# A second inner product of the convolution groups computed in divided form

## The chip, the core and the metric

The kernel runs on one NeuronCore of a Trainium2 chip. TensorE (PE) multiplies matrices into PSUM; its weight loads are shown apart (PEld). VectorE (DVE), ScalarE (ACT) and GpSimd (POOL) work elementwise, and SyncE's queue (SP) issues the DMAs. Engines run beside each other and wait for one another only through semaphores. The metric is the device time of one execution in microseconds, the median of a few runs.

## The reference

One layer of a decoder trunk on 1024 tokens of width 1024, in float32. The projection `h @ w_in` gives twelve blocks of 1024 columns; those of the convolution branch are `c_a`, `x_a`, `z_a`, `b_a`:

```python
u = c_gate * xv
u = conv(u, conv_w) + conv_b      # causal, depthwise, 3 taps over positions
y = b_gate * u * silu(z)
y_a = y @ w_a_out
# beside it: retention over 4 heads, then
merged = sigmoid(g_a) * y_a + sigmoid(g_b) * y_b
x = x + merged @ w_o              # and a final RMSNorm
```

## The kernel before, in words

Every float32 operand is split into a high part (a cast by ScalarE) and a low part (the rest, a subtraction by VectorE), and each product is three matmuls: high x high, high x low, low x high.

The projection runs in 28 value units and then 20 *groups* `g` of channels: groups 0, 1, 18, 19 for gates, 2 to 9 (`CONVS`) for the convolution, 10 to 17 (`turn`) for q and k. A group is a 2x2 block product done with seven products in place of eight, in the order `ORDER = (1, 6, 2, 5, 7, 3, 4)`. Each product is a *unit*: its weights are cast and split into one of three slots (`slots`, taken in turn), so the unit three places later waits until a unit's matmuls are done. A full unit has 24 matmuls of 128x512. GpSimd makes the weight sums of the next group (`s1`, `s3`, `s2`, `s4`) from quadrants that SP loads; product 6 needs S2, and S4 waits for product 6's low part. After each product VectorE adds the PSUM result to running sums (`add`), and the next product in the same banks waits for that (product 5 waits for the addition of 6).

In groups 1 to 18 (`TWICE`) product 4 is itself divided the same way (`second_units`): two half units with 18 and 24 matmuls of 128x256. GpSimd makes four weight sums of 128x256 for the second half (`second_sums`), and VectorE needs four more additions (`second_first`, `second_rest`), because the small products go to several quarters of the result.

For convolution group `g` the elementwise work runs while TensorE is in group `g + 1`: VectorE makes two halves of `u` (`conv_product`; the second half, `conv_product(g, 1)`, still in group g), three taps (`conv_tap`, the first a `TENSOR_SCALAR`), the gating (`conv_y`), and in the group itself an early gate product (`conv_early`) that product 7 waits for; ScalarE makes sigmoids; GpSimd three gate products (`conv_gate`).

The order on each engine is the order in which its loop is written: loops over unit places `u`, in which place `p` of group `g` runs the additions of the unit before, then the high or low part of the unit two places on, then the rest. Nothing reorders it.

Of the kernel before, what the change touches and what calls it, by code (L numbers as in the profile page):

```python
# [6 lines left out]
F32 = mybir.dt.float32  # L7
# [5 lines left out]
P = 128  # L13
# [37 lines left out]
UNIT_TABLE = [(g, p) for g in range(GROUPS) for p in range(8 if g in TWICE else 7)]  # L51
# [54 lines left out]
def ended_at(g):  # L106

    return unit_at(g, 4) + (g in TWICE)


def columns_of(u):

    return 3 * QUARTER if u >= VALUE_UNITS and place_of(u)[0] in TWICE and place_of(u)[1] == 6 else 2 * HALF
# [7 lines left out]
def summed_until(g):  # L121

    return 16 + 4 * g + 4 * len([n for n in TWICE if n < g])


def second_summed(g, n):

    return summed_until(g) + 4 + n


def second_added(g, n):

    return 20 + 4 * (g - TWICE.start) + n
# [138 lines left out]
def build(nc, x_t, columns, w_value, w_channel, w_last, x_rows, final_g, rope, tables, identity, out):  # L272
# [7 lines left out]
    kept_d = nc.dram_tensor("kept_scratch", (P, 2, 2, QUARTER), F32, kind="Internal").ap()  # L280
# [24 lines left out]
    t4_sums = sb("t4_sums", CONS_AT + 8 * KB, [P, 4, 2, QUARTER])  # L305
    v_d, v_b, v_a, v_c = (sb(f"value_{r}", WORK_AT + n * 8 * KB, [P, 2, 1024]) for n, r in enumerate("dbac"))
# [110 lines left out]
    final_in, row_squared, row_var, row_scaled = ident_in, squared, var_made, kept_scaled  # L417

# [33 lines left out]
    def t4_part(n, part):  # L452

        return hc[:, KEPT_AT[4], part, 2 * (n // 2):2 * (n // 2) + 2, n % 2 * QUARTER:(n % 2 + 1) * QUARTER]

    def second_part(name, part):
        return t4_part(1, part) if name == "T3" else hx[:, ("T1", "T2", "T4").index(name), part]

    def second_bank(g):

        return set_at(g + 1, 6)
# [31 lines left out]
    def _(sp):  # L493
# [147 lines left out]
        for part in range(2):  # L641
            sp.dma_start(kept_d[:, part], t4_part(1, part).bitcast(F32)).then_inc(x_in[4], 16)
        for g in range(GROUPS):
            if g + 1 < GROUPS:
# [3 lines left out]
            if g == TWICE.stop:  # L648
                sp.wait_ge(unit_done, ended_at(g - 1) + 1)
                for part in range(2):  # L650
                    sp.dma_start(t4_part(1, part).bitcast(F32), kept_d[:, part]).then_inc(x_in[4], 16)
            if g + 1 < GROUPS:
# [194 lines left out]
    def _(pool):  # L847
# [50 lines left out]
        def second_sums(g):  # L898

            d = work[ROLES[g]["d"]]  # L900
            a11, a12, a22, a21 = (d[:, n * QUARTER:(n + 1) * QUARTER] for n in range(4))
# [1850 lines left out]
```

## Time and profile before

| what | value |
|---|---|
| median of 3 runs | 1368.03 us (1367.47 to 1368.32) |
| profiled execution, first to last instruction | 1366.5 us |
| TensorE, VectorE, ScalarE, GpSimd busy | 99%, 78%, 43%, 35% of the span |
| weight loads busy | 83% |
| granted TensorE clock, mean | 0.999 |

The profile is of one execution. Its view by timeline lists instructions by their start; neighbours of one line are merged, and the bracket says how long the engine was idle before and what ended that. A matmul's shown duration is longer than its distance to the next one, since they are pipelined: read the distances of the starts. On VectorE and ScalarE the next instruction's start is shown a little before the last one's end.

### The profile page before, as it was taken

Reading aid. Unit: us, or ns where it says so; the run is one execution under the profiler, and the core shown is the slowest. Engines: PE = TensorE matmul, PEld = TensorE weight load, DVE = VectorE, ACT = ScalarE, POOL = GpSimd, SP = SyncE. Lnnn points to the kernel's source line nnn. Section 1 sums busy time; section 2 is a strip of 40 time slices with the busy share of each in tenths; the row PEclk is TensorE's granted clock in tenths of the full one; section 3 lists DMA queues with packets and bytes.
Section 4 is the critical chain, followed back from the end, with each engine's and each line's share of the span. In section 5 each row is a group of like instructions: output and inputs, shape, how many; then the busy total and the mean of one; then the engine's idle time right before and its main releaser. Section 6 shows DMA issues by size and latency. Waiting matters only on the chain.

```text
span 1366.5 us, 16902 instructions
## 1 busy us (share of the span) xinstructions
PE 1354.6 (99%) x6498; PEld 1138.4 (83%) x6498; DVE 1063.1 (78%) x1053; ACT 591.4 (43%) x801; POOL 473.3 (35%) x349
## 2 busy tenths in 40 slices
PE   9999999999999999999999999999999999999997
PEld 7888888888888888888888888888888888888886
DVE  6898474578877777788888888747776998788887
ACT  7843233323222233234333333438778434433445
POOL 0100232244555554555555666415454001100002
PEclk9999999999999999999999999999999999999999
DMA  9746313322212222355443444657767699945443
GB/s 338 215 128 216 114 56 124 124 77 77 77 50 63 74 62 62 109 154 154 138 140 124 116 146 141 198 193 254 264 229 261 142 327 312 233 164 200 161 86 124
DMA packets 106128, 212.74 MB, mean 156 GB/s; under 512 B 6977, under 2 KB 49089, under 8 KB 101185
## 3 DMA queue, kind: packets, MB, share of 16 engines
q1 hardware_dynamic: 103024, 193.82, 42.4%
q0 software_dynamic: 2880, 17.83, 6.6%
q8 instruction: 52, 0.85, 0.3%
q14 instruction: 28, 0.22, 0.0%
q10 hardware_dynamic: 144, 0.02, 0.0%
HBM read 148.20 MB, written 55.05 MB: 149 GB/s over the span
## 4 chain that ended last, share of the span: by engine, by line
PE 95%; issue 1%; ACT 1%; DVE 1%; POOL 1%; DMA 0%; SPq 0%; POOLq 0%; DVEq 0%; ACTq 0%
PE psum L2488 16%; PE psum L2489 16%; PE psum L2486 16%; PE psum L2623 7%; PE psum L2625 7%; PE psum L2624 7%; PE psum L2413 4%; PE psum L2415 4%; PE psum L2416 4%; PE psum L2430 2%; PE psum L2432 2%; PE psum L2431 2%; PE psum L2531 2%; PE psum L2533 2%; PE psum L2532 2%
## 5 line engine op out<-in xcount | busy, mean ns | idle before, releaser
L2488 PE MATMUL psum<-hc,slots 128*128 128x512 f32 x976 | 379.8, 389 | 0.0
L2486 PE MATMUL psum<-hc,slots 128*128 128x512 f32 x976 | 379.8, 389 | 0.0
L2489 PE MATMUL psum<-hc,slots 128*128 128x512 f32 x976 | 379.8, 389 | 0.0
L1088 ACT ACTIVATE slots<-work 128x1024 fp32r<-128x1024 f32 (+1 forms) x158 | 162.0, 1036 | 435.9 <-PE psum L2489 329.0
L1583 DVE TENSOR_TENSOR slots<-work,slots 128x1024 fp32r<-128x1024 f32 (+1 forms) x158 | 228.6, 1448 | 39.0 <-ACT slots L1088 39.0
L2489 PEld LDWEIGHTS psum<-hc,slots 128*128 128x128 f32 x976 | 183.2, 188 | 38.1
L2486 PEld LDWEIGHTS psum<-hc,slots 128*128 128x128 f32 x976 | 183.2, 188 | 37.5
L2488 PEld LDWEIGHTS psum<-hc,slots 128*128 128x128 f32 x976 | 183.2, 188 | 37.3
L1348 ACT ACTIVATE last_slot<-arena 128x1024 fp32r<-128x1024 f32 x112 | 118.6, 1062 | 163.0 <-PE psum L2625 156.8
L2623 PE MATMUL psum<-last_slot 128*128 128x512 f32 (+1 forms) x452 | 175.3, 388 | 0.0
L2625 PE MATMUL psum<-last_slot 128*128 128x512 f32 (+1 forms) x452 | 175.0, 387 | 0.0
L2624 PE MATMUL psum<-last_slot 128*128 128x512 f32 (+1 forms) x452 | 175.0, 387 | 0.0
L1900 DVE TENSOR_TENSOR last_slot<-arena,last_slot 128x1024 fp32r<-128x1024 f32 x112 | 135.7, 1222 | 30.4 <-ACT last_slot L1348 29.8
L2624 PEld LDWEIGHTS psum<-last_slot 128*128 128x128 f32 x452 | 84.9, 188 | 17.4
L2625 PEld LDWEIGHTS psum<-last_slot 128*128 128x128 f32 x452 | 84.9, 188 | 17.4
L2623 PEld LDWEIGHTS psum<-last_slot 128*128 128x128 f32 x452 | 84.9, 188 | 17.2
L903 POOL TENSOR_TENSOR work<-work 128x256 f32<-128x256 f32 x18 | 16.3, 906 | 234.7 <-DVE slots L1583 234.7
L2413 PE MATMUL psum<-slots,hc 128*128 128x512 f32 x224 | 88.2, 394 | 1.3 <-DVE slots L1583 1.3
L2416 PE MATMUL psum<-slots,hc 128*128 128x512 f32 x224 | 87.2, 389 | 0.0
L2415 PE MATMUL psum<-slots,hc 128*128 128x512 f32 x224 | 87.2, 389 | 0.0
L878 POOL TENSOR_TENSOR work<-work,work 128x1024 f32<-128x1024 f32 x20 | 48.3, 2414 | 95.8 <-DVE slots L1583 95.8
L1729 DVE TENSOR_TENSOR tp_v<-psum,tp_v 128x1024 f32<-128x1024 f32 x40 | 48.7, 1218 | 35.9 <-PE psum L2489 35.9
(214 smaller groups left out, 2331.2 us busy)
## 6 DMA issues: line engine op xcount, KB each, us to landing
work<-w_channel SPq DMA_DIRECT2D x80, 512.0 KB, 3.7
arena<-w_last SPq DMA_DIRECT2D x19, 1024.0 KB, 7.5
qk<-qk_scratch SPq DMA_DIRECT2D x32, 512.0 KB, 3.4
arena<-w_last POOLq DMA_DIRECT2D x9, 1024.0 KB, 11.4
v_raw<-value_scratch SPq DMA_DIRECT2D x32, 256.0 KB, 3.7
arena<-gate_scratch SPq DMA_DIRECT2D x16, 512.0 KB, 7.1
value_c<-w_value SPq DMA_DIRECT2D x10, 512.0 KB, 4.8
rows_of_x<-x_rows SPq DMA_DIRECT2D x8, 512.0 KB, 8.8
```

What stands on the lines that cost most here:

```text
L1088: nc.scalar.activation(slots[:, u % SLOTS, 0, 0:columns_of(u)], src, ACT.Copy).then_inc(w_hi, 1)
L1583: nc.vector.tensor_tensor(slot[:, 1, :], src, slot[:, 0, :].bitcast(F32), ALU.subtract).then_inc(w_ready, 1)
L1900: nc.vector.tensor_tensor(slot[:, 1, :, :], pair_at(group, product, j), slot[:, 0, :, :].bitcast(F32), ALU.subtract).then_inc(last_ready, 1)
L2413: nc.tensor.matmul(bank, x_high, w_high, start=product in starts and i == 0 and kk == 0, stop=False, skip_group_check=True)
L2415: nc.tensor.matmul(bank, x_high, w_low, start=False, stop=False, skip_group_check=True)
L2416: last = nc.tensor.matmul(bank, x_low, w_high, start=False, stop=i == 1 and kk == 1, skip_group_check=True)
L2486: nc.tensor.matmul(bank, slot[:, 0, w], x_high, start=product in STARTS and j == 0, stop=False, skip_group_check=True)
L2488: nc.tensor.matmul(bank, slot[:, 0, w], x_low, start=False, stop=False, skip_group_check=True)
L2489: last = nc.tensor.matmul(bank, slot[:, 1, w], x_high, start=False, stop=j == 3, skip_group_check=True)
L2623: nc.tensor.matmul(bank, l_high, r_high, start=start, stop=False, skip_group_check=True)
L2624: nc.tensor.matmul(bank, l_high, r_low, start=False, stop=False, skip_group_check=True)
L2625: return nc.tensor.matmul(bank, l_low, r_high, start=False, stop=stop, skip_group_check=True)
```

## The change

In convolution groups (`THIRDS = CONVS`) product 3 is divided as product 4 is. The unit table gets one more place there, `THIRD_HALF`, and the halves alternate: first of 3, first of 4, second of 3, second of 4. `second_units` becomes `first_half` and `second_half`, for either product. GpSimd makes four more weight sums, VectorE four more additions. Before group 2, VectorE and ScalarE make the sums and differences of the quarters of product 3's activations once (`t3_quarter`, `t_sum`, `third_high`, `third_low`, four of each); one quarter is overwritten by them, so SP stores it and loads it back before group 10.

Elementwise work moves: the first tap with the bias goes to ScalarE (`first_tap`); the last tap and the gating go ahead of product 7's low part; `conv_product(g, 1)` goes behind the low part of the next group's product 6; the second sigmoid (`late_gate`) goes ahead of that product's cast. On SP the store of `y` goes ahead of one weight load.

```diff
-UNIT_TABLE = [(g, p) for g in range(GROUPS) for p in range(8 if g in TWICE else 7)]
+THIRDS = CONVS
+LAST_HALF, THIRD_HALF = 7, 8
+UNIT_TABLE = [(g, p) for g in range(GROUPS) for p in (0, 1, 2, 3, 4, 5, 6, THIRD_HALF, LAST_HALF)
+              if (p != THIRD_HALF or g in THIRDS) and (p != LAST_HALF or g in TWICE)]
...
+def third_ended_at(g):
+
+    return VALUE_UNITS + UNIT_TABLE.index((g, THIRD_HALF if g in THIRDS else 5))
+
+
+def halved_product(g, product):
+
+    return product == 4 and g in TWICE or product == 3 and g in THIRDS
+
+
+def product_at(n):
+
+    return 3 if n == THIRD_HALF else ORDER[min(n, 6)]
 
 
...
+            if g == THIRDS.start:
+                stores[kind_of(g - 1)](g - 1)
...
-                sp.wait_ge(w_ready, unit_at(g, 3) + 1)
+                if g in THIRDS and g > THIRDS.start:
+                    stores[kind_of(g - 1)](g - 1)
+                sp.wait_ge(w_ready, third_ended_at(g) + 1)
                 load_work(g + 1, "c", 1)
-            if g:
+            if g and g not in THIRDS:
                 stores[kind_of(g - 1)](g - 1)
...
+            if g in THIRDS:
+                second_sums(g, 3)
             if g in TWICE:
-                second_sums(g)
+                second_sums(g, 4)
...
+        def late_gate(g):
+
+            after(g, 3)
+            nc.scalar.activation(gate_z[:, HALF:T], tp_first[g % 2][:, 1, :], ACT.Sigmoid).then_inc(z_sig, 1)
+
+        def first_tap(g):
+
+            c = g - CONVS.start
+            act.wait_ge(conv_step, 5 * c + 3)
+            if c:
+                act.wait_ge(y_out, 16 * c)
+            nc.scalar.activation(taps[:, :], u_pad[:, 0:T], ACT.Identity, scale=cols[:, KT + c:KT + c + 1],
+                                 bias=cols[:, (1 + CONV) * KT + c:(1 + CONV) * KT + c + 1]).then_inc(conv_step, 1)
 
...
+            if VALUE_UNITS <= u < UNITS and place_of(u)[1] == LAST_HALF and place_of(u)[0] in THIRDS:
+                late_gate(place_of(u)[0])
             if u + 2 < UNITS:
                 high(u + 2)
...
+            if p == 1 and g - 1 in CONVS:
+                first_tap(g - 1)
...
-            if n == 0:
-                if c:
-                    dve.wait_ge(y_out, 16 * c)
-                nc.vector.tensor_scalar(taps[:, :], u_pad[:, 0:T], conv_col(0, c), conv_col(CONV, c), ALU.mult, ALU.add)\
-                    .then_inc(conv_step, 1)
-            else:
-                nc.vector.scalar_tensor_tensor(taps[:, :], u_pad[:, n:n + T], conv_col(n, c), taps[:, :],
-                                               ALU.mult, ALU.add).then_inc(conv_step, 1)
+            nc.vector.scalar_tensor_tensor(taps[:, :], u_pad[:, n:n + T], conv_col(n, c), taps[:, :],
+                                           ALU.mult, ALU.add).then_inc(conv_step, 1)
 
...
-                if n == 6 and g in TWICE:
-                    second_first(g)
-                elif n == 7:
-                    second_rest(g)
+                if n in (5, 6) and halved_product(g, product_at(n)):
+                    second_first(g, product_at(n))
+                elif n == LAST_HALF:
+                    second_rest(g, 4)
                     low(u + 1)
+                    if g in THIRDS:
+                        conv_product(g, 1)
                     add(g, 4)
+                elif n == THIRD_HALF:
+                    second_rest(g, 3)
+                    add(g, 3)
                 elif ORDER[n] not in (1, 2):
                     add(g, ORDER[n])
 
-            if u + 2 < UNITS and (u < VALUE_UNITS or place_of(u)[1] < 7):
+            if u >= VALUE_UNITS and place_of(u)[1] == 2 and place_of(u)[0] - 1 in CONVS:
+                conv_tap(place_of(u)[0] - 1, 2)
+                conv_y(place_of(u)[0] - 1)
+            if u + 2 < UNITS and (u < VALUE_UNITS or place_of(u)[1] != LAST_HALF):
                 low(u + 2)
...
-                        conv_tap(last, 0)
                         conv_tap(last, 1)
-                    if p == 2:
-                        conv_tap(last, 2)
-                        conv_y(last)
...
-                if p == 6:
-                    conv_product(g, 1)
...
+        def first_half(g, product):
+
+            u, z = unit_at(g, product), second_bank(g, product)
             pe.wait_ge(w_ready, u + 1)
-            pe.wait_ge(sum_made, 5 * g + sums_until(ORDER, 7))
-            if g == TWICE.start:
+            pe.wait_ge(sum_made, 5 * g + sums_until(ORDER, before(ORDER, product)))
+            if product == 4 and g == TWICE.start:
                 pe.wait_ge(h_ready, made(3) + 4)
-            product_of_quarters(u, 0, quarter(0), one_six, start=True)
-            product_of_quarters(u, 1, quarter(2), c11)
-            product_of_quarters(u, 2, second("T4"), c21).then_inc(unit_done, 1)
-            pe.wait_ge(w_ready, u + 2)
-            product_of_quarters(u + 1, 2, second("T1"), five, start=True)
-            product_of_quarters(u + 1, 3, second("T3"), seven, start=True)
-            product_of_quarters(u + 1, 1, quarter(3), c12)
-            pe.wait_ge(value_sum, second_added(g, 1))
-            product_of_quarters(u + 1, 0, second("T2"), one_six).then_inc(unit_done, 1)
+            if product == 3:
+                pe.wait_ge(sum_made, 5 * g)
+            if product == 3 and g == THIRDS.start:
+                pe.wait_ge(h_ready, made(3) + 8)
+            product_of_quarters(u, 0, quarter(product, 0), psum[:, z, 0:QUARTER], start=True)
+            product_of_quarters(u, 1, quarter(product, 2), direct_quarter(g, product, 0))
+            product_of_quarters(u, 2, second(product, "T4"), direct_quarter(g, product, 2)).then_inc(unit_done, 1)
+
+        def second_half(g, product):
+
+            u, z = (ended_at(g) if product == 4 else third_ended_at(g)), second_bank(g, product)
+            pe.wait_ge(w_ready, u + 1)
+            product_of_quarters(u, 2, second(product, "T1"), psum[:, z + 1, 0:QUARTER], start=True)
+            product_of_quarters(u, 3, second(product, "T3"), psum[:, z + 1, QUARTER:HALF], start=True)
+            product_of_quarters(u, 1, quarter(product, 3), direct_quarter(g, product, 1))
+            pe.wait_ge(value_sum, second_added(g, product, 1))
+            product_of_quarters(u, 0, second(product, "T2"), psum[:, z, 0:QUARTER]).then_inc(unit_done, 1)
 
...
+            if product == 1 and g - 1 in THIRDS:
+                pe.wait_ge(value_sum, second_added(g - 1, 3, 2))
...
-                if product == 4 and g in TWICE:
-                    second_units(g)
+                if halved_product(g, product):
+                    first_half(g, product)
+                    if product == 4 and g in THIRDS:
+                        second_half(g, 3)
+                    if product == 4:
+                        second_half(g, 4)
```

VectorE at the end of a convolution group, before: from the addition of product 3 (`tp_first<-psum,tp_first`) to the low part of the next group's product 6. `slots` rows are low parts, `tp_v` rows product 4's additions.

```order
L1729 TENSOR_TENSOR tp_first_72<-psum,tp_first_72 128x1024 [waits unit_done]
L1583 TENSOR_TENSOR slots<-work_66,slots 128x1024 [waits w_hi]
L1787 TENSOR_TENSOR u_pad<-tp_first_72,tp_v_76 128x512 [waits sum_made]
L1735 TENSOR_TENSOR tp_v_74<-psum,tp_v_74 128x256 [waits unit_done]
L1748 TENSOR_TENSOR tp_v_74<-psum,tp_v_74 128x768 [waits unit_done]
L1748 TENSOR_TENSOR tp_v_74<-psum,tp_v_74 128x2x256 [waits value_sum]
L1748 TENSOR_TENSOR tp_v_74<-psum,tp_v_74 128x512 [waits value_sum]
L1583 TENSOR_TENSOR slots<-work_66,slots 128x1024 [waits w_hi]
```

The same place now. `tp_first` rows of 256, 768 and 2x256 are product 3's new additions.

```order
L1814 TENSOR_TENSOR tp_first_76<-psum,tp_first_76 128x256 [waits unit_done]
L1662 TENSOR_TENSOR slots<-work_74,slots 128x1024 [waits w_hi]
L1814 TENSOR_TENSOR tp_v_78<-psum,tp_v_78 128x256 [waits unit_done]
L1662 TENSOR_TENSOR slots<-work_73,slots 128x1024 [waits w_hi]
L1827 TENSOR_TENSOR tp_first_76<-psum,tp_first_76 128x768 [waits unit_done]
L1827 TENSOR_TENSOR tp_first_76<-psum,tp_first_76 128x2x256 [waits value_sum]
L1827 TENSOR_TENSOR tp_first_76<-psum,tp_first_76 128x512 [waits value_sum]
L1808 TENSOR_TENSOR tp_first_76<-psum,tp_first_76 128x1024 [waits value_sum,unit_done]
L1827 TENSOR_TENSOR tp_v_78<-psum,tp_v_78 128x768 [waits unit_done]
L1827 TENSOR_TENSOR tp_v_78<-psum,tp_v_78 128x2x256 [waits value_sum]
L1827 TENSOR_TENSOR tp_v_78<-psum,tp_v_78 128x512 [waits value_sum]
L1662 TENSOR_TENSOR slots<-work_73,slots 128x1024 [waits w_hi]
```

One low part (of product 4's second half) and the low part of product 1 stand between three short additions; product 3's four late additions come ahead of product 4's three, and the convolution product (`u_pad`) has left.

VectorE from there to the early gate product, before (`taps` are the taps and the gating, L1798 the first tap):

```order
L1729 TENSOR_TENSOR tp_v_74<-psum,tp_v_74 128x1024 [waits value_sum,unit_done]
L1583 TENSOR_TENSOR slots<-work_68,slots 128x1024 [waits w_hi]
L1790 TENSOR_TENSOR u_pad<-u_pad,tp_v_74 128x512 [waits sum_made]
L1583 TENSOR_TENSOR slots<-work_70,slots 128x1024 [waits w_hi]
L1798 TENSOR_SCALAR taps<-u_pad,cols 128x1024 [waits y_out,conv_step]
L1801 SCALAR_TENSOR_TENSOR taps<-u_pad,cols,taps 128x1024 [waits conv_step]
L1729 TENSOR_TENSOR tp_v_73<-psum,tp_first_71 128x1024 [waits first_kept,unit_done]
L1583 TENSOR_TENSOR slots<-work_67,slots 128x1024 [waits w_hi]
L1801 SCALAR_TENSOR_TENSOR taps<-u_pad,cols,taps 128x1024 [waits conv_step]
L1808 TENSOR_TENSOR taps<-taps,gate_z 128x1024 [waits z_made,conv_step]
L1583 TENSOR_TENSOR slots<-work_66,slots 128x1024 [waits w_hi]
L1780 TENSOR_TENSOR gate_z<-psum,gate_z 128x512 [waits z_sig]
```

The same stretch now:

```order
L1879 TENSOR_TENSOR u_pad<-tp_first_76,tp_v_80 128x512 [waits sum_made]
L1808 TENSOR_TENSOR tp_v_78<-psum,tp_v_78 128x1024 [waits value_sum,unit_done]
L1662 TENSOR_TENSOR slots<-work_71,slots 128x1024 [waits w_hi]
L1882 TENSOR_TENSOR u_pad<-u_pad,tp_v_78 128x512 [waits sum_made]
L1662 TENSOR_TENSOR slots<-work_74,slots 128x1024 [waits w_hi]
L1887 SCALAR_TENSOR_TENSOR taps<-u_pad,cols,taps 128x1024 [waits conv_step]
L1808 TENSOR_TENSOR tp_v_79<-psum,tp_first_77 128x1024 [waits first_kept,unit_done]
L1887 SCALAR_TENSOR_TENSOR taps<-u_pad,cols,taps 128x1024 [waits conv_step]
L1894 TENSOR_TENSOR taps<-taps,gate_z 128x1024 [waits z_made,conv_step]
L1662 TENSOR_TENSOR slots<-work_72,slots 128x1024 [waits w_hi]
L1662 TENSOR_TENSOR slots<-work_73,slots 128x768 [waits w_hi]
L1872 TENSOR_TENSOR gate_z<-psum,gate_z 128x512 [waits z_sig]
```

The convolution product of the second half has come in at the top, the first tap has left, and the last tap and the gating stand ahead of two low parts in place of between them.

## Rows read from the trace of the kernel before

**Rows 1.** The page's first line.

```profile
span 1366.5 us, 16902 instructions
```

**Rows 2.** The page: the chain that ended last, share of the span by engine.

```profile
PE 95%; issue 1%; ACT 1%; DVE 1%; POOL 1%; DMA 0%; SPq 0%; POOLq 0%; DVEq 0%; ACTq 0%
```

**Rows 3.** Windows, one group: us, busy time of PE, PEld, DVE, ACT, POOL, clock, DMA.

```profile
350.43:388.02 37.59, 37.59 (x189) 31.96 (x187) 28.84 (x24) 10.81 (x12) 18.88 (x12) 1.00 0.25 70
```

**Rows 4.** Timeline of PE, a group's end: start us, length us, line, operation, count.

```profile
383.07 0.28 PE L2430 MATMUL psum<-hc,slots 128*128 128x256 f32 x1
...
388.02 0.39 PE L2486 MATMUL psum<-hc,slots 128*128 128x512 f32 x1
```

**Rows 5.** Timeline of PEld in the same stretch.

```profile
387.55 0.19 PEld L2430 LDWEIGHTS psum<-hx,slots 128*128 128x128 f32 x1
```

**Rows 6.** Timeline of DVE, over the same group's end.

```profile
378.97 1.22 DVE L1583 TENSOR_TENSOR slots<-work,slots 128x1024 fp32r<-128x1024 f32 x1
...
388.22 2.41 DVE L1748 TENSOR_TENSOR tp_v<-psum,tp_v 128x768 f32<-128x768 f32 x3 [1.08 <-PE psum L2432]
390.54 1.22 DVE L1583 TENSOR_TENSOR slots<-work,slots 128x1024 fp32r<-128x1024 f32 x1
391.68 1.22 DVE L1729 TENSOR_TENSOR tp_v<-psum,tp_v 128x1024 f32<-128x1024 f32 x1
392.81 2.56 DVE L1583 TENSOR_TENSOR slots<-work,slots 128x1024 fp32r<-128x1024 f32 x1
395.30 1.78 DVE L1790 TENSOR_TENSOR u_pad<-u_pad,tp_v 128x512 f32<-128x512 f32 x1
397.00 2.31 DVE L1583 TENSOR_TENSOR slots<-work,slots 128x1024 fp32r<-128x1024 f32 x1
399.23 1.78 DVE L1798 TENSOR_SCALAR taps<-u_pad,cols 128x1024 f32<-128x1024 f32 x1
401.05 1.29 DVE L1801 SCALAR_TENSOR_TENSOR taps<-u_pad,cols,taps 128x1024 f32<-128x1024 f32 x1
402.25 1.22 DVE L1729 TENSOR_TENSOR tp_v<-psum,tp_first 128x1024 f32<-128x1024 f32 x1
```

**Rows 7.** Timeline of POOL, the same stretch.

```profile
374.56 0.74 POOL L903 TENSOR_TENSOR work<-work 128x256 f32<-128x256 f32 x1 [11.70 <-DVE slots L1583]
...
380.36 2.39 POOL L878 TENSOR_TENSOR work<-work,work 128x1024 f32<-128x1024 f32 x1 [2.86 <-DVE slots L1583]
382.71 2.41 POOL L883 TENSOR_TENSOR work<-work,work 128x1024 f32<-128x1024 f32 x1
386.28 2.78 POOL L889 TENSOR_TENSOR work<-work,work 128x1024 f32<-128x1024 f32 x1 [1.16 <-DVE slots L1583]
391.89 2.40 POOL L896 TENSOR_TENSOR work<-work,work 128x1024 f32<-128x1024 f32 x1 [2.83 <-DVE slots L1583]
394.24 2.28 POOL L922 TENSOR_TENSOR gate_z<-gate_z,tp_first 128x512 f32<-128x512 f32 x1
396.49 1.74 POOL L926 TENSOR_TENSOR gate_z<-gate_z,tp_v 128x512 f32<-128x512 f32 x1
```

**Rows 8.** Timeline of ACT, the same stretch.

```profile
377.83 1.06 ACT L1088 ACTIVATE slots<-work 128x1024 fp32r<-128x1024 f32 x1 [4.59 <-PE psum L2489]
...
389.15 2.01 ACT L1088 ACTIVATE slots<-work 128x1024 fp32r<-128x1024 f32 x2 [3.99 <-POOL work L889]
```

**Rows 9.** Timeline of DVE, early in the kernel.

```profile
36.35 2.66 DVE L1638 SCALAR_TENSOR_TENSOR hc<-raw_b,cols,hc 128x512 fp32r<-128x512 f32 x2
...
40.07 1.40 DVE L1638 SCALAR_TENSOR_TENSOR hc<-raw_b,cols,hc 128x512 fp32r<-128x512 f32 x2
```

**Rows 10.** Timeline of POOL, early in the kernel.

```profile
35.39 2.41 POOL L936 TENSOR_TENSOR value_d<-value_b,value_d 128x1024 f32<-128x1024 f32 x1
```

**Rows 11.** Timeline of PE where it waited, early in the kernel.

```profile
13.09 0.50 PE L2413 MATMUL psum<-slots,hc 128*128 128x512 f32 x1 [1.32 <-DVE slots L1583]
13.43 0.40 PE L2415 MATMUL psum<-slots,hc 128*128 128x512 f32 x1
```

More of the change, by code:

```diff
@@ L121, in summed_until, with second_summed, second_added @@
 def summed_until(g):
[L123 to L133, printed above, removed]
+    return 16 + 4 * g + 4 * len([n for n in TWICE if n < g]) + 4 * len([n for n in THIRDS if n < g])
+def second_summed(g, product, n):
+    return summed_until(g) + 4 + 4 * (product == 4 and g in THIRDS) + n
+def second_added(g, product, n):
+    before_g = 20 + 4 * (g - TWICE.start) + 4 * len([f for f in THIRDS if f < g])
+    if g not in THIRDS:
+        return before_g + n
+    return before_g + (1 + (product == 4) if n == 1 else 1 + n + 3 * (product == 4))
 def before(order, product):
@@ L1465, in _ @@
                 second_high("T3")
+            if g == THIRDS.start and p == 2:
+                third_high("T2")
+                third_high("T4")
+                third_high("T3")
+            if g == THIRDS.start and p == 4:
+                third_high("T1")
             if 0 < g <= GROUPS:
@@ L1493, in _ @@
                     gate(g, tp_first, 3)
-            if kind == "conv" and p == 6:
-                after(g, 3)
-                nc.scalar.activation(gate_z[:, HALF:T], tp_first[g % 2][:, 1, :], ACT.Sigmoid).then_inc(z_sig, 1)
             if g == GROUPS - 1:
@@ L2018, in _ @@
                 second_low("T3")
+            if g == THIRDS.start - 1 and p in (1, 2):
+                for n in range(2):
+                    t3_quarter(2 * (p - 1) + n)
+            if g == THIRDS.start - 1 and p in (4, 5):
+                for name in (("T1", "T3"), ("T2", "T4"))[p - 4]:
+                    t_sum(name, t3_quarters, t3_sums, 20)
+            if g == THIRDS.start and p == 3:
+                for name in ("T2", "T4", "T3"):
+                    third_low(name)
+            if g == THIRDS.start and p == 4:
+                third_low("T1")
             if g == CONVS.start and p == 0:
@@ L2417, in value_unit @@
             last.then_inc(unit_done, 1)
-        def second_units(g):
-            u, x, z = unit_at(g, 4), set_at(g, 4), second_bank(g)
-            c11, c12, c21 = (psum[:, x + n // 2, n % 2 * QUARTER:(n % 2 + 1) * QUARTER] for n in range(3))
-            one_six, five, seven = psum[:, z, 0:QUARTER], psum[:, z + 1, 0:QUARTER], psum[:, z + 1, QUARTER:HALF]
-            def product_of_quarters(unit, place, right, to, start=False):
-                slot = slots[:, unit % SLOTS]
-                for j in range(2):
-                    w = slice((2 * place + j) * P, (2 * place + j + 1) * P)
-                    high, low = (right(part)[:, j, :] for part in range(2))
-                    nc.tensor.matmul(to, slot[:, 0, w], high, start=start and j == 0, stop=False, skip_group_check=True)
-                    nc.tensor.matmul(to, slot[:, 0, w], low, start=False, stop=False, skip_group_check=True)
-                    last = nc.tensor.matmul(to, slot[:, 1, w], high, start=False, stop=j == 1, skip_group_check=True)
-                return last
-            def quarter(n):
-                return lambda part: t4_part(n, part)
-            def second(name):
-                return lambda part: second_part(name, part)
@@ new lines, in product_of_quarters @@
+        def product_of_quarters(unit, place, right, to, start=False):
+            slot = slots[:, unit % SLOTS]
+            for j in range(2):
+                w = slice((2 * place + j) * P, (2 * place + j + 1) * P)
+                high, low = (right(part)[:, j, :] for part in range(2))
+                nc.tensor.matmul(to, slot[:, 0, w], high, start=start and j == 0, stop=False, skip_group_check=True)
+                nc.tensor.matmul(to, slot[:, 0, w], low, start=False, stop=False, skip_group_check=True)
+                last = nc.tensor.matmul(to, slot[:, 1, w], high, start=False, stop=j == 1, skip_group_check=True)
+            return last
@@ L2441, in second_units, with direct_quarter, quarter, second @@
+        def direct_quarter(g, product, n):
+            return psum[:, set_at(g, product) + n // 2, n % 2 * QUARTER:(n % 2 + 1) * QUARTER]
+        def quarter(product, n):
+            return lambda part: x_quarter(product, n, part)
+        def second(product, name):
+            return lambda part: second_part(product, name, part)
+        def first_half(g, product):
+            u, z = unit_at(g, product), second_bank(g, product)
             pe.wait_ge(w_ready, u + 1)
[L2442 removed]
```

141 lines of the change are left out of this document (92 added, 49 removed).

## The prediction

> **What bounds the kernel now.** I read the page's span and chain first: 1366.5 us [rows 1], and 95% of the chain that ended last is TensorE [rows 2]. Then the stage that the change touches, one convolution group at a time, in the view by windows: in the group from 350.43 to 388.02 us TensorE is busy for the whole 37.59 us at a granted clock of 1.00, the 2.4 GHz level, VectorE for 28.84, GpSimd 18.88, ScalarE 10.81 [rows 3]. So a microsecond of matmul taken out of these groups is a microsecond of time, as long as no other engine comes late; and the question is how late the others already are. That is in the timelines of VectorE, GpSimd and ScalarE around a group's end [rows 6 to 8], and most of this text goes through them.
>
> **What the matmuls give back.** Product 4 is already divided: it starts at 383.07 and the next group's product 1 at 388.02, so its 42 matmuls of 256 columns take 4.95 us, 0.118 each [rows 4]: 2.12 for the 18 of the first half, 2.83 for the 24 of the second. The other six products share 37.59 - 4.95 = 32.64 us, 5.44 each (24 matmuls of 512 columns, 0.227 us each). Product 3 divided as product 4 is costs 4.95 in place of 5.44: 0.49 us a group, 8 groups, 3.9 us. A group without waits would last 37.11 us, with its halves ending at 29.33 (3, first), 31.45 (4, first), 34.28 (3, second) and 37.11 (4, second), counted from its first matmul.
>
> Whether 18 more weight loads a group eat this: one starts at 387.55 and lasts 0.19 us [rows 5], while matmuls there follow each other by 0.118 us, so loads lie under matmuls and the 0.49 stands. The Trainium skill (TensorE: Matmul & The Clock Gate, The mechanism) says that a weight load overlaps running matmuls only where it goes to other rows of the array; by that rule and the page's 128 columns at 1.2 per ns, an estimate, 18 x 0.107 = 1.9 us a group would be added and the change would lose 11 us; the trace, with full 128x128 loads hidden, disagrees.
>
> **How the other engines take turns.** The trace shows that a VectorE instruction with two operands in SBUF and a GpSimd instruction don't run together: each runs to its end while the other is held, and they alternate. The low part at 392.81 took 2.56 us, against 1.22 two rows earlier; GpSimd's fourth sum ran until 394.29, and 394.29 + 1.08 = 395.37 is its end [rows 6, 7]. GpSimd's first gate product, from 394.24, then ended 1.15 after that (396.52), the convolution product at 395.30 0.56 after that (397.08), and so on through the next gate product (396.49), the low part at 397.00, a third gate product and the first tap at 399.23. VectorE's additions from PSUM (1.22 at 391.68 beside the fourth sum) are not held. For the taps that stay on VectorE (scalar_tensor_tensor) no row of this stage shows a hold, but earlier two instructions of that kind took 2.66 us from 36.35 while GpSimd ran from 35.39 to 37.80, against 1.40 for two at 40.07 [rows 9, 10]. So I hold them too. An instruction that was held ends about 0.15 sooner after the release than it would alone (1.08 for 1.22), so I use 2.25 for a held sum of 2.40, and 0.7 alone for the convolution product that ran 0.56.
>
> **The walk through a group's end.** Latencies from the rows: 0.20 us from a product's end to what it releases (388.02 to 388.22), 0.08 from a cast to its low part (377.83 + 1.06 to 378.97), 0.17 from a low part to GpSimd (378.97 + 1.22 to 380.36), 0.09 from GpSimd to a cast; an engine's next instruction starts 0.08 before the last one's shown end [rows 6 to 8]. From the group's first matmul:
>
> 3's four new sums (0.74 each) follow its first half's low part, from 21.3 to 24.3, and 4's end by 28.2; the second half of 3, cast from 27.41, has its low part by 29.8 and is wanted at 31.45: covered. The second half of 4 needs its slot from 3's first half: cast 29.54 to 30.60 (1.06), low part to 31.90. Before, this low part ended at 29.8 (0.17 before GpSimd's S1 at 380.36), two microseconds earlier, because its slot came from product 7. It starts S1: 32.07 to 34.47. The next product 1's low part, ready at 32.81, is held by S1, runs to 35.55 and holds S3, which ends at 37.80; S2 runs to 40.15 (before, it ended 1.04 us after the group's end, now 3.04 after). The cast for product 6 follows, 40.24 to 41.30; the late sigmoid, put ahead of it, waits for 3's addition (39.03) and is done by then. VectorE meanwhile: 3's four additions from 35.47 (2.32 + 1.14), 4's three to 41.3. Product 6's low part is 41.38 to 42.60. TensorE wants to start product 6 at 37.11 + 5.44 = 42.55. After a late low part it starts some 0.04 later (no row here; the other engines need 0.08 to 0.17) and loses another 0.11 on the first matmul (13.09 to 13.43 is 0.34, not 0.23) [rows 11]: 42.75, a **wait of 0.20 us** where there was none.
>
> From there VectorE: the second half's convolution product, moved behind this low part, 42.52 to 43.20, holding S4 (due 42.77), which then ends at 45.45; 4's addition (PSUM) to 44.34; low part 2, held by S4, to 46.53 (TensorE wants it at 48.19: covered); gate 47.68; first half's convolution product 48.24; gate 49.39; low part 5 50.47; last gate 51.62. The first tap is gone from here (1.78 before, of which it ran 0.55). On ScalarE it has no row; a cast of the same 128x1024 takes 1.06, the tap on VectorE took 1.78; either way, started at 48.28, it ends by 50.06, and the second tap is not due before 50.39, so I cost it at nothing. Second tap, held by the last gate, to 51.62 + 1.15 = 52.77; then 6's addition, 52.69 to 53.91. TensorE may not start product 5 before that addition, and wants to at 42.75 + 10.88 = 53.63. With 0.15 as above: 54.06, a **wait of 0.43 us**. Before, this addition ended at 403.47, 15.45 after the group's start, 0.87 ahead of need. So it is not the added instructions as such (three additions like 4's 2.41 and a low part, less the first tap: some 3 us a group on an engine that idles 8.7) but their place.
>
> Bounds: the second tap, if GpSimd doesn't hold it, ends at 51.6, and the second wait is gone (0). If one more turn is lost to GpSimd it grows to about 0.8. I take 0.43, by the rows of the hold at 36.35. The last tap and gating, moved ahead of product 7's low part, end it at 57.4; TensorE wants product 7 at 59.5: covered, as is the early gate product (58.9). Weight loads on SP stand behind moved stores: the y store now ahead of a load waits for work done at 19 us of a group, the load for a low part at 29.8, so nothing moves; in the first such group the gate stores go ahead of a load that is needed 25 us later. Four 256 KB copies for product 3's kept quarter pass under matmuls.
>
> **Once only.** In the first convolution group three new low parts (128x512, 0.7 each as above) stand ahead of the early gate product and alternate with the four new sums of 0.74 [rows 7]; that puts it at about 21.93 where product 7 is due at 21.76: 0.3 us. Earlier work for the quarters lies in group 1, where VectorE has no convolution: nothing.
>
> **Sum.** -8 x 0.49 + 8 x (0.20 + 0.43) + 0.3 = -3.9 + 5.0 + 0.3 = +1.4 us: span 1367.9. The runs' median lies 1.5 us above the profiled span, which I carry over: 1369.5 us. What can be told from no change is 0.2%, 2.7 us; this is inside.
>
> **Rivals.**
> Neither wait appears (0.15). The misses are small against what they are made of: product 6's low part is late by 0.20 with the refill, 6's addition by 0.43, at the end of chains of ten and twenty instructions. If VectorE and GpSimd together run 0.5 us earlier than I have them, the whole 3.9 us stay: 1364.1. Against it: the turns are read off rows to 0.05 us.
> Only the first wait (0.20). If the second tap isn't held, or GpSimd's last gate comes before low part 5: -3.9 + 1.6 + 0.3 = -2.0, 1366.0. Against it, [rows 9, 10].
> Slower (0.18): S4 takes its turn before the moved convolution product. Both are released by the end of product 6's low part, VectorE's own by 0.25 us earlier; if it loses, it runs after S4 (45.17) to 45.73, 4's addition goes to 46.87, low part 2 to 47.96, low part 5 behind the last gate to 51.9, the second tap to 53.1, 6's addition to 54.25: 0.34 more in each group, 2.7 in all, 1372.2. It decides from a delay of 0.25 us on VectorE. For it: the margin is a quarter of a microsecond after twenty steps; against it: at 386.28 S2, due at once after a low part, was held by just such a product (2.78 against 2.40) [rows 7].
> That the change doesn't do what it says: if the 18 more weight loads of a group lay bare at 0.19 us each, 3.4 us a group would be lost and the time be 1391. Product 4's 42 matmuls at 0.118 us, shorter than one load, exclude it [rows 4, 5]: no chance.
>
> **Numbers.** Forecast 0.47, own range 1367.3 to 1371.3 (0.1 us of error at either wait is 0.8 us in eight groups). Faster by over 0.2%: nearly all of the first rival and a little of the second, 0.18. Slower: most of the last and a little of the forecast, 0.19. Within: 0.63. Range 1364.5 to 1372.0, which leaves out the far halves of the outer rivals.
>
> **What would show it.** In the profile after: groups of about 37.7 us, not 37.1; TensorE idle before product 6, put down to VectorE's low part, and before product 5, put down to VectorE's addition, some 0.1 to 0.4 us eight times each, where before there was nothing; S2 ending 3 us after the group's end; low part of product 1 at 2.5 us or more, held by S1; S3 at 3.4. If groups are 37.1 long and TensorE never idles, the walk was too slow; if the waits stand at another product, its order is wrong.

## The result, and the profile after

The changed kernel takes 1370.54 us (median of 21 runs, 1370.04 to 1371.49) against 1368.28 us for the kernel before (21 runs, 1367.47 to 1369.34): a ratio of 1.0016, 95% interval 1.0010 to 1.0023. That is 2.3 us slower, under the 0.2% that the prediction took for what can't be told from no change, though the interval leaves a ratio of 1 out: a small loss. 1369.5 us was forecast, with a range of 1364.5 to 1372.0. The page of the profiled execution begins with the span, and its chain of waits by engine answers to [rows 2]:

```profile
span 1368.9 us, 17315 instructions
...
PE 83%; DVE 11%; issue 2%; ACT 2%; POOL 1%; DMA 0%; SPq 0%; POOLq 0%; DVEq 0%; ACTq 0%
```

TensorE's share of the chain fell from 95% to 83% and VectorE's rose from 1% to 11%. TensorE hardly idles for it: the chain goes over to the engine that released a late matmul and follows that engine's work back through a part of a group. Read such a share as "VectorE now arrives last somewhere", not as 11% of lost time. The window of one group, as in [rows 3], gives the size:

```profile
351.14:388.95 37.81, 37.63 (x206) 32.34 (x205) 32.53 (x29) 12.78 (x14) 22.67 (x16) 1.00 0.22 71
```

37.81 us, not 37.59, with the clock still at 1.00 (the 2.4 GHz level). TensorE's busy time, 37.63, is short of the window by only 0.18: the rest of what it loses lies inside matmuls that run longer. The timeline of TensorE shows both places (start, length, line, operation):

```profile
356.37 0.39 PE L2602 MATMUL psum<-hc,slots 128*128 128x512 f32 x1
356.65 0.50 PE L2599 MATMUL psum<-hc,slots 128*128 128x512 f32 x1
356.99 0.39 PE L2601 MATMUL psum<-hc,slots 128*128 128x512 f32 x1
...
367.44 0.39 PE L2602 MATMUL psum<-hc,slots 128*128 128x512 f32 x1
368.00 0.47 PE L2599 MATMUL psum<-hc,slots 128*128 128x512 f32 x1 [0.18 <-DVE tp_v L1808]
368.31 0.40 PE L2601 MATMUL psum<-hc,slots 128*128 128x512 f32 x1
...
378.98 0.28 PE L2523 MATMUL psum<-hc,slots 128*128 128x256 f32 x1
...
388.95 0.39 PE L2599 MATMUL psum<-hc,slots 128*128 128x512 f32 x1
```

Starts are read, not idle times. Undisturbed starts stand 0.227 apart. Before product 6 they stand 0.28 and 0.34 apart (356.37, 356.65, 356.99): 0.17 us lost, with no idle time in brackets at all. Before product 5 they stand 0.56 and 0.31 apart: 0.42 lost, of which the brackets show 0.18 and name VectorE's addition. Both recur in each group from 281 to 557 us (0.16 to 0.17 lost at product 6, 0.37 to 0.42 at product 5). The last two rows bound the four halves: 84 matmuls in 9.97 us.

VectorE over the same group's end, the rows that answer to [rows 6]:

```profile
344.61 1.22 DVE L1662 TENSOR_TENSOR slots<-work,slots 128x1024 fp32r<-128x1024 f32 x1 [0.55 <-ACT slots L1132]
...
346.75 2.74 DVE L1662 TENSOR_TENSOR slots<-work,slots 128x1024 fp32r<-128x1024 f32 x1 [0.58 <-ACT slots L1132]
349.42 2.40 DVE L1827 TENSOR_TENSOR tp_first<-psum,tp_first 128x768 f32<-128x768 f32 x3
351.92 1.23 DVE L1808 TENSOR_TENSOR tp_first<-psum,tp_first 128x1024 f32<-128x1024 f32 x1
353.06 2.40 DVE L1827 TENSOR_TENSOR tp_v<-psum,tp_v 128x768 f32<-128x768 f32 x3
355.38 1.22 DVE L1662 TENSOR_TENSOR slots<-work,slots 128x1024 fp32r<-128x1024 f32 x1
356.51 0.69 DVE L1879 TENSOR_TENSOR u_pad<-tp_first,tp_v 128x512 f32<-128x512 f32 x1
357.11 1.22 DVE L1808 TENSOR_TENSOR tp_v<-psum,tp_v 128x1024 f32<-128x1024 f32 x1
358.25 2.30 DVE L1662 TENSOR_TENSOR slots<-work,slots 128x1024 fp32r<-128x1024 f32 x1
...
364.41 2.31 DVE L1887 SCALAR_TENSOR_TENSOR taps<-u_pad,cols,taps 128x1024 f32<-128x1024 f32 x1
366.64 1.21 DVE L1808 TENSOR_TENSOR tp_v<-psum,tp_first 128x1024 f32<-128x1024 f32 x1
367.78 1.27 DVE L1887 SCALAR_TENSOR_TENSOR taps<-u_pad,cols,taps 128x1024 f32<-128x1024 f32 x1
```

GpSimd in the same stretch, to be laid beside them as [rows 7] beside [rows 6]: S1, S3, S2, S4 and the last of the three gate products.

```profile
346.01 2.41 POOL L920 TENSOR_TENSOR work<-work,work 128x1024 f32<-128x1024 f32 x1 [4.66 <-DVE slots L1662]
348.37 3.39 POOL L925 TENSOR_TENSOR work<-work,work 128x1024 f32<-128x1024 f32 x1
351.72 2.42 POOL L931 TENSOR_TENSOR work<-work,work 128x1024 f32<-128x1024 f32 x1
356.73 2.73 POOL L938 TENSOR_TENSOR work<-work,work 128x1024 f32<-128x1024 f32 x1 [2.59 <-DVE slots L1662]
...
363.49 2.15 POOL L971 TENSOR_TENSOR gate_z<-gate_z,tp_v 128x512 f32<-128x512 f32 x1
```

The low part at 346.75 takes 2.74 us because S1 runs until 348.42; S3, from 348.37, takes 3.39 because that low part runs until 349.49; and the second tap at 364.41 takes 2.31 where the third, with GpSimd idle, takes 1.27. The additions from PSUM (2.40 for three, 1.22 for one) are not held. No semaphore makes these waits: they lie inside instructions that have already started. So it is not true of VectorE and GpSimd, as the first section has it, that engines wait for one another only through semaphores.

Laid on the walk of the prediction with the group's end as the common point (351.14 here, 37.11 there): S2 ends at 40.11, 40.15 forecast; product 6's low part at 42.57, 42.60 forecast; product 6's addition at 53.82, 53.91 forecast; TensorE starts product 5 at 53.97, 54.06 forecast.

### The profile page after: what moved, and what is told of

Read it like the earlier page. It is cut to its first block, busy times and chain, and to the rows that moved or that the text cites. A ratio compares the mean times of both kernels' runs of the same rounds, so it can differ in the third digit from the quotient of the medians.

```text
span 1368.9 us, 17315 instructions
## 1 busy us (share of the span) xinstructions
PE 1355.9 (99%) x6642; PEld 1142.2 (83%) x6642; DVE 1104.5 (81%) x1097; ACT 608.9 (44%) x821; POOL 506.8 (37%) x381
## 4 chain that ended last, share of the span: by engine, by line
PE 83%; DVE 11%; issue 2%; ACT 2%; POOL 1%; DMA 0%; SPq 0%; POOLq 0%; DVEq 0%; ACTq 0%
PE psum L2599 13%; PE psum L2601 12%; PE psum L2602 12%; PE psum L2742 7%; PE psum L2740 7%; PE psum L2741 7%; PE psum L2512 4%; PE psum L2514 4%; PE psum L2515 4%; DVE slots L1662 3%; PE psum L2523 2%; PE psum L2525 2%; PE psum L2524 2%; PE psum L2644 2%; PE psum L2646 2%
## 5 line engine op out<-in xcount | busy, mean ns | idle before, releaser
L2599 PE MATMUL psum<-hc,slots 128*128 128x512 f32 x912 | 356.7, 391 | 1.2 <-DVE tp_v L1808 0.4
L2601 PE MATMUL psum<-hc,slots 128*128 128x512 f32 x912 | 355.2, 389 | 0.0
L2602 PE MATMUL psum<-hc,slots 128*128 128x512 f32 x912 | 355.0, 389 | 0.0
L1132 ACT ACTIVATE slots<-work 128x1024 fp32r<-128x1024 f32 (+1 forms) x166 | 168.5, 1025 | 341.8 <-PE psum L2602 213.2
L1662 DVE TENSOR_TENSOR slots<-work,slots 128x1024 fp32r<-128x1024 f32 (+1 forms) x166 | 243.9, 1474 | 47.1 <-ACT slots L1132 47.1
L2599 PEld LDWEIGHTS psum<-hc,slots 128*128 128x128 f32 x912 | 171.2, 188 | 41.8 <-issue 4.8
L2602 PEld LDWEIGHTS psum<-hc,slots 128*128 128x128 f32 x912 | 171.2, 188 | 36.0
L2601 PEld LDWEIGHTS psum<-hc,slots 128*128 128x128 f32 x912 | 171.2, 188 | 34.2
L945 POOL TENSOR_TENSOR work<-work 128x256 f32<-128x256 f32 x26 | 23.4, 899 | 200.6 <-DVE slots L1662 200.6
```

The lines of the kernel that those rows point to most:

```text
L1132: nc.scalar.activation(slots[:, u % SLOTS, 0, 0:columns_of(u)], src, ACT.Copy).then_inc(w_hi, 1)
L1662: nc.vector.tensor_tensor(slot[:, 1, :], src, slot[:, 0, :].bitcast(F32), ALU.subtract).then_inc(w_ready, 1)
L2599: nc.tensor.matmul(bank, slot[:, 0, w], x_high, start=product in STARTS and j == 0, stop=False, skip_group_check=True)
L2601: nc.tensor.matmul(bank, slot[:, 0, w], x_low, start=False, stop=False, skip_group_check=True)
L2602: last = nc.tensor.matmul(bank, slot[:, 1, w], x_high, start=False, stop=j == 3, skip_group_check=True)
```

## The experiments

All are edits of the changed kernel, timed on a chip beside the kernel before (1368.3 to 1368.4 us there).

**The second tap behind product 6's addition**, in the place of the third, which it now precedes:

```
-                    if p == 1:
-                        conv_tap(last, 1)
...
+                conv_tap(place_of(u)[0] - 1, 1)
                 conv_tap(place_of(u)[0] - 1, 2)
```

> VectorE's second tap stands behind product 6's addition (and ahead of the third tap) instead of ahead of it; nothing else changes. Theory (the place of the tap makes the wait): the wait before product 5, 0.42 us in each of eight groups of the changed kernel, goes, the wait before product 6 (0.19 us) stays: 1370.5 - 3.4 = 1367.2 us, groups of 37.4 us. Rival (VectorE and GpSimd have too much work in a group): the wait only moves to product 7, whose low part and early gate product now come behind two taps; 1370.5 us, TensorE idle before product 7 by about 0.4 us in each group.

1367.21 us; ratio to before 0.9992 (0.9983 to 1.0000). The wait before product 5 is gone, the one before product 6 stays, and nothing appears at product 7. VectorE now, with both taps behind the addition in the last row:

```profile
365.49 1.21 DVE L1808 TENSOR_TENSOR tp_v<-psum,tp_first 128x1024 f32<-128x1024 f32 x1
366.63 2.59 DVE L1887 SCALAR_TENSOR_TENSOR taps<-u_pad,cols,taps 128x1024 f32<-128x1024 f32 x2
```

So the place of one tap cost 3.3 us, not the amount of work; the rival that the wait only moves to product 7 falls.

**S1 on VectorE.** GpSimd's S1 is left out for groups behind a convolution group, and VectorE makes it; GpSimd's S3 waits for that. The place on VectorE:

```
...
                     second_first(g, product_at(n))
+                    if product_at(n) == 4 and g in THIRDS:
+                        s1(g + 1)
...
```

> In the convolution groups the first sum for the next group (S1) is made by VectorE, behind the first addition of product 4, in place of GpSimd. Theory (both waits hang on the chain low part of 4b, S1, low part of the next product 1, S3, S2): S1 takes VectorE 1.2 us where it now stands held for 1.4 us; the next product 1's low part takes 1.2 to 1.3 us and not 2.74; everything behind it, product 6's low part and addition too, comes about 1.0 us earlier; both waits go, 8 x 0.61 us: 1365.6 us, groups of 37.2 us. Rival 1 (the second wait has a cause of its own, the held tap): only the wait before product 6 goes, 1369.0 us. Rival 2 (1.2 us more on the engine that comes late): VectorE ends a group later than now, 1371.5 us or more.

1365.57 us; ratio 0.9980 (0.9971 to 0.9989): 5.0 us less than the changed kernel, from 1.2 us *more* work a group on the engine that came late. VectorE, from S1 on:

```profile
345.18 1.21 DVE L1838 TENSOR_TENSOR work<-work,work 128x1024 f32<-128x1024 f32 x1
346.31 1.22 DVE L1666 TENSOR_TENSOR slots<-work,slots 128x1024 fp32r<-128x1024 f32 x1
347.61 2.41 DVE L1831 TENSOR_TENSOR tp_first<-psum,tp_first 128x768 f32<-128x768 f32 x3
...
353.58 1.21 DVE L1666 TENSOR_TENSOR slots<-work,slots 128x1024 fp32r<-128x1024 f32 x1
...
364.84 1.21 DVE L1812 TENSOR_TENSOR tp_v<-psum,tp_first 128x1024 f32<-128x1024 f32 x1
```

The low part behind S1 takes 1.22 in place of 2.74. Counted from the end of the group (350.23 here), product 6's low part starts at 3.35, 4.24 before, and product 6's addition at 14.61, 15.50 before. TensorE's matmuls stand undisturbed before both products. So both waits hang on one chain; the rival that gives them two causes falls, though one can be removed alone, as the tap showed.

**The last gate product cut short.** It works on one of its 512 columns; the rest is left out.

```
-                nc.gpsimd.tensor_tensor(late, late, tp_v2[m][:, 1, :], ALU.mult)
+                nc.gpsimd.tensor_tensor(late[:, 0:1], late[:, 0:1], tp_v2[m][:, 1, 0:1], ALU.mult)
```

> GpSimd's last gate product of each convolution group is cut to 1 of its 512 columns, so most of that product is left out of the result. Theory (a tap, scalar_tensor_tensor, is held by a GpSimd instruction that runs): the second tap takes 1.27 us as the third does, not 2.31, product 6's addition ends 1.0 us earlier, the wait before product 5 (0.42 us) goes: 1367.2 us. Rival (this tap is slow by itself, for what it reads was just written): it stays at 2.3 us and the time at 1370.5 us.

1367.57 us; ratio 0.9994 (0.9985 to 1.0003). The wait before product 5 is gone. The same tap, in the same place and reading the same data:

```profile
363.69 1.27 DVE L1887 SCALAR_TENSOR_TENSOR taps<-u_pad,cols,taps 128x1024 f32<-128x1024 f32 x1
```

It is GpSimd that held it. What was read off [rows 9, 10], from other shapes early in the kernel, holds here.

**The first tap back on VectorE.**

```
                     if p == 1:
+                        conv_tap(last, 0)
                         conv_tap(last, 1)
...
```

> The first tap and bias go back from ScalarE to VectorE, ahead of the second tap; the rest of the change stays. Theory (VectorE's row ahead of product 6's addition decides): that addition comes later by the tap, 0.6 us alone to 1.8 us as held in the kernel before; the wait before product 5 grows from 0.42 us to 1.0 to 2.2: 1375 to 1384 us. Rival (the row is not what the wait hangs on): 1370.5 us.

1377.46 us; ratio 1.0064 (1.0052 to 1.0077). The added tap (1.78) takes the hold on itself, and the second one then runs free (1.28):

```profile
366.52 1.78 DVE L1888 TENSOR_SCALAR taps<-u_pad,cols 128x1024 f32<-128x1024 f32 x1
368.33 1.28 DVE L1891 SCALAR_TENSOR_TENSOR taps<-u_pad,cols,taps 128x1024 f32<-128x1024 f32 x1
369.54 1.22 DVE L1806 TENSOR_TENSOR tp_v<-psum,tp_first 128x1024 f32<-128x1024 f32 x1
```

So it costs 1.78 + 1.28 - 2.31 = 0.75 us before that addition, and the groups are 0.79 us longer on average: near the lower end of what was expected. Moving the first tap to ScalarE was worth 6.9 us here by the medians, of which eight groups make 6.3.

**The moves without the division.** The set of groups with a divided product 3 is made empty; the moves keep a set of their own.

```
-THIRDS = CONVS
+MOVED = CONVS
+THIRDS = range(GROUPS + 9, GROUPS + 9)
...
```

> Product 3 is not divided (no new halves, sums or quarters), all moves of the change stay: first tap on ScalarE, moved convolution product, late sigmoid ahead of the cast, last tap and gating ahead of product 7's low part, moved stores. Theory (the waits come from the division's own additions and from S1's later start, not from the moves): TensorE never idles, groups of 37.6 us as before, 1368.3 us. Rival (the moves make the waits themselves): 0.4 to 0.6 us a group remain, 1371.5 to 1373 us.

1368.25 us; ratio 0.9999 (0.9990 to 1.0007). The window of one group reads as before, with 1.1 us less VectorE work than in [rows 3]:

```profile
349.86:387.45 37.59, 37.59 (x188) 31.97 (x188) 27.75 (x23) 12.01 (x13) 18.87 (x12) 1.00 0.22 70
```

The moves neither cost nor gain by themselves; the waits come with the division.

**S3 cut short.** S1, S3 and S2 follow each other on GpSimd; here S3 works on one column, after a wait for S1; the rest of that sum is left out.

```
+            if g - 1 in THIRDS:
+                pool.wait_ge(summed, summed_until(g) + 1)
+                a, b = a[:, 0:1], b[:, 0:1]
             nc.gpsimd.tensor_tensor(b, a, b, ALU.subtract).then_inc(summed, 1)
...
```

> GpSimd's third sum S3 for the groups that follow a convolution group is cut to 1 of its 1024 columns, so product 7 is left wrong there; it stands between S1 and S2 on GpSimd. Theory (two chains end together at product 6's low part: S1, S3, S2 and the cast at 355.3, and VectorE's own additions of the two second halves at 355.46): S2 ends 3 us earlier, the low part starts as late as before, both waits stay, 1370.5 us. Rival (the low part waits for S2's cast alone): it starts 0.5 us or more earlier, the wait before product 6 goes and the one before product 5 shrinks as much, 1366 to 1368.5 us.

1370.88 us; ratio 1.0018 (1.0009 to 1.0027): no gain, and both waits stay. S2, on GpSimd, now ends at 351.60, 2.0 us earlier against the group's end (3 were expected), and its cast, behind the late sigmoid, at 354.27; but the low part still starts where VectorE's additions of the second halves end, 4.24 behind the group's end (350.64 here) as in the changed kernel:

```profile
348.06 0.99 POOL L928 TENSOR_TENSOR work<-work,work 128x1 f32<-128x1 f32 x1
349.19 2.41 POOL L934 TENSOR_TENSOR work<-work,work 128x1024 f32<-128x1024 f32 x1
```

```profile
352.56 2.40 DVE L1830 TENSOR_TENSOR tp_v<-psum,tp_v 128x768 f32<-128x768 f32 x3
354.88 1.22 DVE L1665 TENSOR_TENSOR slots<-work,slots 128x1024 fp32r<-128x1024 f32 x1
```

In the changed kernel two chains end together at that low part, the cast behind S2 (354.23 + 1.06; the row below merges it with the next cast) and VectorE's own row (353.06 + 2.40): shortening one gives nothing. S1 on VectorE shortened both, since the held low part stands at the head of both. ScalarE in the changed kernel:

```profile
354.23 2.01 ACT L1132 ACTIVATE slots<-work 128x1024 fp32r<-128x1024 f32 x2 [0.41 <-POOL work L931]
```

**The moved convolution product back ahead of product 6's low part.**

```
+                    if g in THIRDS:
+                        conv_product(g, 1)
                     low(u + 1)
-                    if g in THIRDS:
-                        conv_product(g, 1)
```

> The second half's convolution product goes back ahead of product 6's low part on VectorE; the rest of the change stays. Theory (row and turns as in the walk): the low part comes 0.66 us later and the wait before product 6 grows from 0.19 to about 0.85; S4 is then not held by that product, so product 6's addition comes only about 0.35 later and the wait before product 5 shrinks from 0.42 to about 0.1: 0.36 us more a group, 1373.4 us. Rival (the two orders cost the same): 1370.5 us.

1372.84 us; ratio 1.0031 (1.0019 to 1.0043). TensorE at product 6:

```profile
319.08 0.39 PE L2602 MATMUL psum<-hc,slots 128*128 128x512 f32 x1
319.96 0.50 PE L2599 MATMUL psum<-hc,slots 128*128 128x512 f32 x1 [0.49 <-DVE slots L1662]
```

Starts 0.88 apart and the longer first matmul make some 0.77 before product 6, against 0.17; before product 5 about 0.1 remains. The five undivided products take 28.11 us in place of 27.84: 0.27 a group, 0.36 expected.

**Two things done once.** With S1 on VectorE, the four sums for product 3's quarters were all put at product 7's place in group 1 (in the trace they stand behind the low part of product 4's first half), and the early gate product ahead of the three new low parts in the first convolution group. The first of the two:

```
-            if g == THIRDS.start - 1 and p in (4, 5):
-                for name in (("T1", "T3"), ("T2", "T4"))[p - 4]:
+            if g == THIRDS.start - 1 and p == 4:
+                for name in ("T1", "T3", "T2", "T4"):
...
```

> The kernel with S1 on VectorE, and two edits of things done once: the four sums for product 3's quarters all stand behind product 7's low part in group 1 (two of them stood one product later and delayed the first half's addition of product 4), and in the first convolution group the early gate product stands ahead of the three new low parts. Theory: TensorE's gaps at 236.9 (0.71 us) and at 259.9 (0.26 us) go: 1365.57 - 0.97 = 1364.6 us. Rival (the work only delays something else in those two groups): 1365.6 us.

1365.21 us; ratio 0.9977 (0.9969 to 0.9986). The gap at 259.9 went, the one at 236.3 stayed: half a miss. GpSimd and VectorE there:

```profile
223.72 1.11 POOL L949 TENSOR_TENSOR work<-work 128x256 f32<-128x256 f32 x1 [23.39 <-DVE slots L1666]
...
233.20 2.41 POOL L929 TENSOR_TENSOR work<-work,work 128x1024 f32<-128x1024 f32 x1
```

```profile
223.56 1.83 DVE L1860 TENSOR_TENSOR t_sums<-t_quarters 128x512 f32<-128x512 f32 x2
...
233.57 3.13 DVE L1666 TENSOR_TENSOR slots<-work,slots 128x1024 fp32r<-128x1024 f32 x1
236.62 0.41 DVE L1818 TENSOR_TENSOR tp_v<-psum,tp_v 128x256 f32<-128x256 f32 x1
```

The quarters' sums now take turns with GpSimd's four sums (1.11 for 0.74); S1 and S3 follow from there, and S3 holds the low part at 233.57 for its whole length. The addition at 236.62, which TensorE waits for, stands behind it. So the sums were put one product earlier still, where GpSimd is idle (against the last edit):

```
-            if g == THIRDS.start - 1 and p == 4:
+            if g == THIRDS.start - 1 and p == 3:
```

> As the kernel before it (S1 on VectorE, the early gate product ahead of the new low parts), but the four sums for product 3's quarters stand one product earlier in group 1, before GpSimd's four new sums for product 4 start at 223.7. Theory (the gap at 236.3 hangs on GpSimd: its four sums, S1 and S3 came 0.9 us later because they took turns with the quarters' sums, and S3 then held the next low part for 3.13 us): the low part takes 1.8 us as in the kernel before, the gap of 0.73 us goes, 1365.2 - 0.7 = 1364.5 us. Rival (the division of product 3 makes that gap by some other way, such as the stores moved on SP): it stays, 1365.2 us.

1364.78 us; ratio 0.9974 (0.9964 to 0.9984): faster than both kernels, by 3.5 us than the one before. The low part takes 1.80 and the addition comes 0.9 us earlier; TensorE loses nothing in this stage, and a group is as long as its matmuls:

```profile
234.00 1.80 DVE L1666 TENSOR_TENSOR slots<-work,slots 128x1024 fp32r<-128x1024 f32 x1
235.72 0.41 DVE L1818 TENSOR_TENSOR tp_v<-psum,tp_v 128x256 f32<-128x256 f32 x1
```

```profile
349.15:386.34 37.19, 37.19 (x207) 32.50 (x205) 31.90 (x30) 12.77 (x14) 20.20 (x15) 1.00 0.22 72
```

## Why the prediction was right, and where it was off

**What binds: right.** TensorE, as long as nobody is late; the moves alone left the time where it was.

**The turns of VectorE and GpSimd: right.** The held durations of the walk are in the trace within 0.1 us, the tap included, and the short gate product shows who holds it. The first tap on ScalarE, which had no row and was put at nothing, takes 1.25 us and ends 0.9 us before the second.

**The waits: right in place and size.** 0.20 + 0.43 = 0.63 us a group were forecast. The five undivided products take 27.84 us here and 27.21 to 27.22 where no wait is left (S1 on VectorE): 0.63. Eight groups lose 5.0 us. One sign failed: no idle time shows before product 6, only the distances of the starts.

**What the matmuls give back: mis-sized.** 0.49 us a group was forecast, by doubling product 4's 4.95. The four halves take 9.97, not 9.90, and a group without waits 37.19, not 37.11. Against [rows 3] the gain is 0.40 a group, 3.2 us in place of 3.9. The 84 matmuls follow each other by 0.1187 us, product 4's 42 alone by 0.1179. The starts in the traces say where: the 18 matmuls that read `hx`, the sums that belong to product 4, follow each other by 0.1165 us, the other 66 by 0.1193; in the kernel before, product 4 alone has 18 at 0.1162 and 24 at 0.1189. Product 3's 42 read no `hx`, so they take 5.0 us and not 4.95. Why the ones with `hx` are quicker is open; no run was made for it.

**The weight loads: right.** Bare at 0.19 us each, 18 more would cost 3.4 us a group; all that the halves took beyond the doubled 4.95 is 0.07. The Trainium skill (TensorE: Matmul & The Clock Gate, The mechanism) says in one line that a weight load overlaps running matmuls only where it goes to other rows of the array; no run here bears that out. The same section of the Trainium skill also has loads into a background weight buffer pulled ahead of matmuls, which no run here tests.

**Once only: one term right, one missed.** The early gate product delays product 7 of the first convolution group by 0.27 us (0.3 forecast). But "Earlier work for the quarters lies in group 1 [...]: nothing" was wrong. TensorE, in the second half of product 4 in group 1:

```profile
236.48 0.28 PE L2525 MATMUL psum<-hc,slots 128*128 128x256 f32 x1
237.19 0.39 PE L2523 MATMUL psum<-hx,slots 128*128 128x256 f32 x1 [0.43 <-DVE tp_v L1814]
237.41 0.28 PE L2524 MATMUL psum<-hx,slots 128*128 128x256 f32 x1
```

0.71 and 0.22 where 0.118 is the usual distance: 0.7 us lost. TensorE waits for VectorE's addition at 236.72. Ahead of that, the second pair of quarter sums takes 3.49 us beside S1 and S3, where two such sums with GpSimd idle take 1.41 (the last run):

```profile
229.97 3.49 DVE L1849 TENSOR_TENSOR t_sums<-t_quarters,t_sums 128x512 f32<-128x512 f32 x2
```

I had asked whether VectorE has room there (it has), and not whom its instructions hold on GpSimd.

**The sum.** -3.2 + 5.0 + 0.3 + 0.7 = +2.8 us for this stage, against +1.4 forecast; the spans differ by 2.4 (1368.9 - 1366.5), so some 0.4 lies the other way elsewhere (0.3 of it before this stage: product 4 of group 1 starts at 232.37 and not 232.69), and the medians by 2.3. The two misses, 0.7 each, have one sign; that the total came out nearer than they make it is luck.

**The rivals.** "Neither wait", "only the first wait" and the bare weight loads fall by the trace. "Slower: S4 goes ahead of the moved convolution product" didn't happen: the product runs at 356.51 and S4, due behind the same low part, is held to 2.73. The time came out slower by a part of that rival's amount, and for another reason.

## What to carry to other kernels

When two engines can't run at once, an instruction's price is its own time plus what it makes the other one late; ask of every piece, one-off work too, which instruction of the other engine stands due beside it. A sum that starts a chain may be cheaper on the busier engine: it cost VectorE 1.2 us, spared it a hold of 1.5, and brought forward all that stood behind. And where two chains end within 0.2 us of each other at one instruction, look for what stands at the head of both before shortening either.

## What the runs showed of the hardware

A GpSimd instruction on a single column still waits its turn: S3 on one column, from 348.06, took 0.99 us, the last gate product on one column 1.05, each ending 0.05 to 0.06 us behind the shown end of the VectorE instruction that was running (348.99 and 363.76). What such an instruction takes beside an idle VectorE no run shows. And a late TensorE loses more than the trace counts as idle: at product 6, late by 0.05 us (356.65 for 356.37 + 0.227), the first matmul lasted 0.50 and not 0.39, so 0.17 was lost with nothing in the brackets.
